# Mixture of experts: scatter and gather in halves between a neighbouring expert's units, h cast on ACT

## The reference, cut to what matters

```python
def _moe_swiglu(x, w_router, b_router, w_gate, w_up, w_down):
    logits = (x @ w_router).astype(jnp.float32) + b_router.astype(jnp.float32)
    top_vals, top_idx = lax.top_k(logits, TOP_K)          # TOP_K = 2
    top_w = jax.nn.softmax(top_vals, axis=-1)
    combine = jnp.sum(jax.nn.one_hot(top_idx, N_EXPERTS, dtype=jnp.float32) * top_w[..., None], axis=-2)
    out = jnp.zeros_like(x)
    for e in range(N_EXPERTS):                            # N_EXPERTS = 8
        out = out + combine[..., e:e + 1].astype(x.dtype) * _swiglu(x, w_gate[e], w_up[e], w_down[e])
    return out
```

## Time and profile before

| | us |
|---|---|
| median of 3 runs | 3123.27 |
| lowest and highest | 3120.66, 3128.55 |
| span of the profiled execution | 3126.1 |
| busy: PE, DVE, ACT | 2690.1, 2311.1, 1477.0 |
| start of the expert layer (first gather) to its last scatter | 1978 to 3108 |

### The profile page before, as it was taken

How to read it: one execution, slowest core, us unless ns; L and a number is a source line. 1 busy time by engine, 2 the same in 40 slices (tenths; PEclk the granted TensorE clock), 3 DMA queues, 4 the chain that set the end, 5 groups by cost and what they waited for, 6 DMA issues and landing times.

```text
span 3126.1 us, 48237 instructions
## 1 busy us (share of the span) xinstructions
PE 2690.1 (86%) x17714; PEld 2431.0 (78%) x17715; DVE 2311.1 (74%) x2670; ACT 1477.0 (47%) x1605; POOL 950.9 (30%) x566
## 2 busy tenths in 40 slices
PE   7998689899888987568996656799999989998997
PEld 7987489899888886347996534698888979897896
DVE  5666466667668656867777686698888979897897
ACT  4333443433343333125552212476666767666665
POOL 6960069599209002317996321000000000000000
PEclk9988699899898998688997778799999999999999
DMA  7753157477344442025752203497978969896985
GB/s 279 253 182 142 41 215 257 172 257 255 134 182 141 168 161 106 27 101 210 261 207 85 101 31 118 158 359 299 343 277 298 361 261 359 307 363 258 344 310 195
DMA packets 128885, 670.36 MB, mean 214 GB/s; under 512 B 14496, under 2 KB 14688, under 8 KB 79632
## 3 DMA queue, kind: packets, MB, share of 16 engines
q1 hardware_dynamic: 110848, 604.72, 52.6%
q0 software_dynamic: 17936, 64.18, 5.9%
HBM read 667.80 MB, written 1.05 MB: 214 GB/s over the span
## 4 chain that ended last, share of the span: by engine, by line
PE 78%; DVE 14%; issue 3%; ACT 3%; POOL 1%; DMA 1%; DVEq 0%; SPq 0%; ACTq 0%
PE work L1372 15%; PE work L1373 15%; PE work L1374 15%; PE acc L1372 9%; PE acc L1373 8%; PE acc L1374 8%; PE acc L1720 1%; PE work L1712 1%; DVE scratch L1049 1%; PE acc L1735 1%; PE work L1420 1%; DVE wl_gu L644 1%; PE work L1449 1%; DVE xT_lo L731 1%; DVE wl_gu L1142 1%
## 5 line engine op out<-in xcount | busy, mean ns | idle before, releaser
L1372 PE MATMUL work<-xT_hi,wh_gu 128*128 128x256 f32 x2120 | 613.6, 289 | 54.9 <-DVE xT_lo L731 19.6
L1373 PE MATMUL work<-xT_lo,wh_gu 128*128 128x256 f32 x2120 | 611.2, 288 | 0.0
L1374 PE MATMUL work<-xT_hi,wl_gu 128*128 128x256 f32 x2120 | 610.2, 288 | 0.0
L1372 PE MATMUL work<-wh_gu,mixT_hi 128*128 128x256 f32 x1792 | 510.3, 285 | 10.5 <-DVE wl_gu L1142 9.7
L1373 PE MATMUL work<-wl_gu,mixT_hi 128*128 128x256 f32 x1792 | 505.9, 282 | 0.0
L1374 PE MATMUL work<-wh_gu,mixT_lo 128*128 128x256 f32 x1792 | 505.8, 282 | 0.0
L644 DVE TENSOR_TENSOR wl_gu<-raw_gu,wh_gu 128x2048 fp32r<-128x2048 f32 x158 | 394.8, 2499 | 133.9 <-ACT wh_gu L351 133.3
L1372 PEld LDWEIGHTS work<-xT_hi,wh_gu 128*128 128x128 f32 x2120 | 417.9, 197 | 66.5 <-DVE xT_lo L731 21.9
L1373 PEld LDWEIGHTS work<-xT_lo,wh_gu 128*128 128x128 f32 x2120 | 418.3, 197 | 4.7
L1374 PEld LDWEIGHTS work<-xT_hi,wl_gu 128*128 128x128 f32 x2120 | 417.9, 197 | 0.0
L1372 PE MATMUL acc<-wh_d,h_hi 128*128 128x512 f32 x912 | 382.2, 419 | 4.1 <-DVE wl_d L1147 4.1
(11 more groups left out here) (417 smaller groups left out, 4942.1 us busy)
## 6 DMA issues: line engine op xcount, KB each, us to landing
raw_gu<-in_w_gu SPq DMA_DIRECT2D x271, 1024.0 KB, 4.9
raw_d<-in_w_d SPq DMA_DIRECT2D x269, 512.0 KB, 5.3
scratch<-in_w_gu SPq DMA_DIRECT2D x112, 1024.0 KB, 7.1
scratch<-in_w_d SPq DMA_DIRECT2D x112, 512.0 KB, 7.9
scratch<-in_w_mod POOLq DMA_DIRECT2D x96, 512.0 KB, 3.7
scratch<-in_s_b POOLq DMA_DIRECT2D x16, 256.0 KB, 3.0
rows<-in_norm_post POOLq DMA_DIRECT2D x6, 512.0 KB, 3.9
rows<-in_ln_g POOLq DMA_DIRECT2D x4, 512.0 KB, 4.0
```

The costliest lines, as they stand in the source:

```text
L1372: pe.matmul(out_, w[0], m[0], start=start, stop=False)
L1373: pe.matmul(out_, w[0], m[1], start=False, stop=False)
L1374: return pe.matmul(out_, w[1], m[0], start=False, stop=stop)
```

## The change

**PE.** The transposes and the scatter of the predecessor move into the expert: `scatter_previous(e, 0)` behind unit 3, `(e, 1)` behind unit 5, the transposes behind unit 7. The gather for the next expert is cut into two halves behind units 16 and 17. Scatter, transposes and gather now all use banks 2 and 3 of `work`. Behind gate_up(27) follow h_transpose(26), down(25), h_transpose(27), down(26), down(27) without anything between. The counts of both experts of a pair are loaded at the top of the pair loop. More units are written out: 0 to 7 and 16 to 19, with loops of 2 x 4 between and behind them.

**ACT** takes over the cast of h (`h_hi`), between silu and the cast of the gate and up weights. `gathered` comes in halves, behind units 17 and 18. At the end it does `moe_hi_d(27)`, the h cast, `moe_hi_gu(29)`.

**DVE** loses that cast in the sparse form; adds a scattered half behind units 3 and 5 (`add_scattered`), copies the weights behind unit 7 (`keep_weights`) and makes the low part of the tokens in halves behind units 18 and 19. The one-hot matrices are made at the top of an expert as before, those with weights for e instead of e + 1. The semaphores count halves. Before the loop there is no scatter of zeros any more; it falls on units 3 and 5 of expert 0. The final scatter is as before.

The diff, cut to the sparse form; the dense form gets the same insertions behind units 1, 2, 3 and 16 to 19.

```diff
@@ ACT @@
+            def gathered(i, half, e=0):
+
+                done = 2 * e + (2 * i + half + 1)
+                act.wait_ge(moe_s["gathered"], done)
...
+                for k in range(4 * half, 4 * half + 4):
...
+                act.activation(XGH[i % 2][:, 4 * half:4 * half + 4, :], XGF_K[:, 4 * half:4 * half + 4, :],
+                               ACT.Copy).then_inc(moe_s["xg_h"], 1)
...
+                def h_hi(i, at):
+
+                    k = (N0 + i) % 2
+                    act.wait_ge(moe_s["hT"], at + (i + 1))
+                    act.activation(HH[k][:, 0:P], PA[:, 2 + k, 0:P], ACT.Copy).then_inc(moe_s["hh"], 1)
+
+                def sparse_step(i, at, first=False):
+
+                    silu(i, at, P)
+                    if not first:
+                        h_hi(i - 1, at)
                     if i < NF2 - 1:
                         moe_hi_gu(i + 2, at)
                         moe_hi_d(i, at)
-                    else:
+
+                def sparse(e, r, pair):
+                    at = e * NF2
+                    sparse_step(0, at, first=True)
+                    for i in range(1, 8):
+                        sparse_step(i, at)
+                    with act.Fori(0, 2) as j:
+                        for i in range(8, 12):
+                            sparse_step(i, at + j * 4)
+                    sparse_step(16, at)
+                    sparse_step(17, at)
+                    gathered(r + 1, 0, pair * 2)
+                    sparse_step(18, at)
+                    gathered(r + 1, 1, pair * 2)
+                    sparse_step(19, at)
+                    with act.Fori(0, 1) as j:
+                        for i in range(20, 24):
+                            sparse_step(i, at + j * 4)
+                    for i in range(24, NF2):
+                        sparse_step(i, at)
+                    moe_hi_d(NF2 - 1, at)
+                    h_hi(NF2 - 1, at)
+                    moe_hi_gu(NF2 + 1, at)
@@ DVE @@
-                def split(i, at, src, width):
+                def h_lo(i, at, src, width):
 
                     k = (N0 + i) % 2
-                    dve.tensor_copy(HH[k][:, 0:width], src).then_inc(moe_s["hh"], 1)
                     dve.wait_ge(moe_s["hh"], at + (i + 1))
...
+                def add_scattered(e, t):
+
+                    dve.wait_ge(moe_s["scattered"], 2 * e + (t + 1))
+                    dve.wait_ge(moe_s["acc"], 2 * e + (t + 1))
+                    TT(ACC[:, t, :], ACC[:, t, :], tile2(PB[:, 2:4, :]), ALU.add).then_inc(moe_s["acc"], 1)
+
+                def keep_weights(e):
+                    dve.wait_ge(moe_s["wT"], e + 1)
+                    dve.tensor_copy(WGT_T, PB[:, 2, 0:S]).then_inc(moe_s["wT_sb"], 1)
...
+                    for i in range(1, 9):
+                        sparse_step(i, at)
+                        if i in (3, 5):
+                            add_scattered(e, (i - 3) // 2)
+                        if i == 7:
+                            keep_weights(e)
+                    with dve.Fori(0, 2) as j:
+                        for i in range(9, 13):
                             sparse_step(i, at + j * 4)
-                    for i in range(NF2 - 3, NF2):
+                    for i in range(17, 21):
+                        sparse_step(i, at)
+                        if i in (18, 19):
+                            xg_lo(r + 1, i - 18, pair * 2)
+                    for i in range(21, NF2):
                         sparse_step(i, at)
@@ PE @@
+                def scatter_previous(e, t):
+
+                    if t == 0:
+                        pe.wait_ge(moe_s["y"], e + 1)
+                        pe.wait_ge(moe_s["wT_sb"], e + 1)
+                    else:
+                        pe.wait_ge(moe_s["acc"], 2 * e + 2)
+                    scatter(t, PB[:, 2:4, :]).then_inc(moe_s["scattered"], 1)
+
+                def weights_transpose(e):
+                    pe.wait_ge(moe_s["onehots"], e + 2)
+                    pe.wait_ge(moe_s["acc"], 2 * e + 3)
...
+                    step(3, at)
+                    scatter_previous(e, 0)
+                    step(4, at)
+                    step(5, at)
+                    scatter_previous(e, 1)
+                    step(6, at)
+                    step(7, at)
+                    weights_transpose(e)
+                    with pe.Fori(0, 2) as j:
+                        for i in range(8, 12):
+                            step(i, at + j * 4)
+                    step(16, at)
+                    pe.wait_ge(moe_s["wT_sb"], e + 2)
+                    gather(0)
+                    step(17, at)
+                    gather(1)
+                    step(18, at)
+                    step(19, at)
+                    with pe.Fori(0, 2) as j:
+                        for i in range(20, 24):
+                            step(i, at + j * 4)
                     h_transpose(NF2 - 1, at)
                     slot_down(NF2 - 2, at, False, False)
                     slot_down(NF2 - 1, at, False, True)
...
                 with pe.Fori(0, NE // 2) as pair:
+                    counts = [pe.value_load(members[:, bass.ds(pair * 2 + r, 1)], min_val=0, max_val=S)
+                              for r in range(2)]
                     for r in range(2):
                         e = pair * 2 + r
-                        pe.wait_ge(moe_s["onehots"], e + 2)
-                        for t in range(NT):
-                            last = pe.transpose(PB[:, (N0 + 1) % 2, (2 + t) * P:(3 + t) * P], WGT[:, t], ident)
-                        last.then_inc(moe_s["wT"], 1)
-                        pe.wait_ge(moe_s["y"], e + 1)
-                        pe.wait_ge(moe_s["wT_sb"], e + 1)
-                        scatter()
-                        pe.wait_ge(moe_s["xg_l"], e + 1)
-                        count = pe.value_load(members[:, bass.ds(e, 1)], min_val=0, max_val=S)
-                        with pe.If(count <= P):
+                        pe.wait_ge(moe_s["xg_l"], 2 * e + 2)
+                        with pe.If(counts[r] <= P):
                             sparse(e, r)
```

More of the change, by code:

```diff
@@ L582, in moe, with silu @@
                 moe_hi_gu(1)
-                gathered(0)
-                def step(i, at, width):
+                gathered(0, 0)
+                gathered(0, 1)
+                def silu(i, at, width):
                     n = N0 + i
@@ L593, in step, with dense @@
+                def dense(e, r, pair):
+                    at = e * NF2
+                    def step(i, at):
+                        silu(i, at, S)
+                        moe_hi_gu(i + 2, at)
                         moe_hi_d(i, at)
-                        moe_hi_gu(i + 2, at)
-                def steps(e, width):
-                    with act.Fori(0, NF2 // 4 - 1) as j:
+                    with act.Fori(0, 4) as j:
                         for i in range(4):
-                            step(i, e * NF2 + j * 4, width)
-                    for i in range(NF2 - 4, NF2):
-                        step(i, e * NF2, width)
+                            step(i, at + j * 4)
+                    for i in range(16, 20):
+                        step(i, at)
+                        if i in (17, 18):
+                            gathered(r + 1, i - 17, pair * 2)
+                    with act.Fori(0, 2) as j:
+                        for i in range(20, 24):
+                            step(i, at + j * 4)
@@ L603, in moe @@
                 with act.Fori(0, NE // 2) as pair:
+                    counts = [act.value_load(members[:, bass.ds(pair * 2 + r, 1)], min_val=0, max_val=S)
+                              for r in range(2)]
                     for r in range(2):
                         e = pair * 2 + r
-                        count = act.value_load(members[:, bass.ds(e, 1)], min_val=0, max_val=S)
-                        with act.If(count <= P):
-                            steps(e, P)
-                            gathered(r + 1, pair * 2)
+                        with act.If(counts[r] <= P):
+                            sparse(e, r, pair)
@@ L612, in moe @@
                         with act.Else():
-                            steps(e, S)
-                            gathered(r + 1, pair * 2)
+                            dense(e, r, pair)
             act.wait_ge(cols_in, 16)
@@ L1151, in moe @@
                 moe_lo_gu(1)
[L1152 to L1153 removed]
+                xg_lo(0, 0)
+                xg_lo(0, 1)
                 def gated(i, at, width):
@@ L1795, in dense @@
-                    wide_gate_up(3, at)
-                    wide_down(2, at, False, False)
-                    with pe.Fori(0, (NF2 - 4) // 4) as j:
-                        for i in range(4, 8):
-                            wide_gate_up(i, at + j * 4)
-                            wide_down(i - 1, at + j * 4, False, False)
-                    pe.wait_ge(moe_s["onehots"], e + 3)
-                    gather()
+                    wide_gate_up(1, at)
+                    pe.wait_ge(moe_s["y"], e + 1)
```

(16 more changed lines are left out.)

139 lines of the change are left out of this document (70 added, 69 removed).

## The result

The kernel after takes 3148.16 us at the median (3143.53 to 3151.22), the kernel before 3123.73 beside it. The ratio is 1.0067, 95% interval 1.0050 to 1.0084: slower by 0.67%, some 21 us. The profiled execution has a span of 3149.4, 23.3 more than before's 3126.1. The traces shown were taken at a mean granted clock of 0.91 to 0.92; only that of e12 was at 0.635, in a run of 3961 us, which is left out of its time.

A forecast was written before the change was run, and what follows sets the result against it. PE bounds the kernel inside experts and waits for code between them; seams inside pairs +3.2, loop-backs +8.4, last tail +1.0 and start -3.0 gave +9.6 us, so 3133 us, range 3111 to 3150.

The forecast's parts named there:

- forecast case: Whole kernel: the summed terms hold and the time is 3125 to 3141 us; chance 0.50.
- code stalls of ACT and DVE: Rival at the seams: ACT's and DVE's longer written-out code makes them wait for code too, 3146 us; chance 0.16.
- idle time before the first gate_up: PE between experts: 2.26 us inside a pair and 9.46 at loop-backs kept, plus 0.1 and 2.0 added.
- half clock behind it: PE's slow clock after a seam's idle time: 1.1 us inside a pair, 1.75 at a loop-back.
- tail stalls: PE at an expert's end waits for `wl_d`, 0.7 us before down(26) and 0.8 before down(27).
- gather, scatter, transposes in the stream: Pieces moved between PE's units still cost 7.3 us an expert, plus 0.2 for a late silu: 7.5.
- cast on ACT: Each sparse unit: h's cast moved from DVE to ACT costs zero, with 0.9 us of cover left.
- first gather to the first expert's third gate_up: Start of the expert layer: gate_up(2) comes at 1997.0 instead of 2003.94, -6.9 us.
- the value loads: Top of PE's pair loop: two exposed loads of the counts, with the wait and the If, +2.0 us each loop-back.
- The shorter code stall: Rival at PE's loop-back: the code fetch costs only as much as the jump and the clock stays up, 3112 us; chance 0.13.
- The clock did not stay up: Rival at the seams: the clock stays up after the shorter seams, 3123 to 3127 us, no change; chance 0.15.
- late in every unit: Rival in each unit: ACT or DVE becomes late for PE, 3155 us at 0.1 us past the cover; chance 0.06.

The follow-up runs named there:

- e12: e9 with PE told the jump's target two units before each expert's end: 0.9922 of the kernel before.
- e7: Kernel before with only the sparse units' cast of h moved from DVE to ACT, one step late: ratio 1.0006 to the kernel before.
- e5: Kernel after, SP holding loads from unit 4 of each next expert until PE did its first gate_up tile: 0.9998 of the kernel before.
- e6: Kernel before with the same hold of SP's loads as e5: 0.9969 of the kernel before.
- e3: Kernel before with ACT's and DVE's sparse units written out instead of looped, PE untouched: 0.9999 of the kernel before.
- e10: Kernel after with PE's loop over pairs of experts written out and e5's hold of SP's loads: 0.9937 of the kernel before.
- e8: Kernel before with PE's loop over pairs of experts written out four times: 0.9938 of the kernel before.
- e2: Kernel after with the branch and the dense form taken out on ACT and DVE, PE keeping it: 1.0060 of the kernel before.
- e4: Kernel after with PE's value load once an expert, behind its wait for tokens, instead of two per pair: 1.0087 of the kernel before.
- e9: Kernel after with PE's loop over pairs of experts written out four times: 0.9995 of the kernel before.
- e11: e8 with PE told the jump's target ahead of the tail's gather: 0.9854 of the kernel before, median 3085.6 us.

## Why the prediction was right in sign and small in size

The forecast was 3133 and +9.6 us; measured were 3148 and +23.3 between the profiles. That 3148 lies in the stated range of 3111 to 3150 is in part luck: the forecast case ended at 3141, and the upper end was set for a rival (code stalls of ACT and DVE) that turned out not to be the cause. Point by point, between the third gate_up of the first expert and that of the last (seven periods, before 975.0, after 1002.2: +27.2, forecast +11.6):

| step | forecast | measured |
|---|---|---|
| idle time before the first gate_up, sum of 7 | +6.4 | +17.8 |
| half clock behind it, sum of 7 | 9.7 in all | 16.4 (before 11) |
| tail stalls, each expert | 0.7 + 0.8 | 0.49 + 0.65 |
| gather, scatter, transposes in the stream | 7.5 | 7.25 |
| cast on ACT | 0 | 0 (e7: ratio 1.0006) |
| steady unit | 4.37 | 4.37 |
| first gather to the first expert's third gate_up | -6.9 | -6.8 (25.5 to 18.8) |
| last expert's third gate_up to the end | +4.9 | +6.5 (147.1 to 153.6) |

The three stretches add up to the 26.9 (-6.8, +27.2, +6.5). Inside an expert PE stayed the bound: from 2137 to 2250 in after it is busy for all of the 113.00 us at PEclk 1.00, DVE for 98.36 and ACT for 81.52. Slips of the forecast's arithmetic are small beside this: 1.1 for the clock is called a mean of 0 and 1.7, which is 0.85; the loop-backs' +8.4 is 8.2 by its own figures; and the start of the very first gate_up, 1985.09 + 1.5 + 0.6 + 0.65, is 1987.8, not 1988.1.

**The step that failed** is the sentence "2.26 and 9.46 idle are kept. Nothing covers them." The mechanism behind it (PE waits for code, and moving the scatter doesn't change that) was right; the term was mis-sized. I took a duration of the jump from before as if it belonged to the branch. It belonged to the branch *at an idle DMA*, and the change took away what made the DMA idle there. The rows held a hint: the kernel before had a window at DMA 0.34 over the loop-back seam, which the prediction notes and does not use. That window is too wide to show more, since it takes in the jump with its quiet queues and the loop-back with full ones. Inside the pairs idle time came to 4.68, 4.01, 3.37 and 3.74 where 2.3 was forecast: 15.8 in sum against 8.3 before, 7.1 more than the 0.4 I had added. At the loop-backs 13.0 to 13.5 came: 10.3 more than before, where I had added 6.0. That makes the 11.4 us that the idle term lacked. The loop-back's own branch did not grow, and the 2.0 for the value loads fit what e5 and e6 leave between them (1.7). What was missing is the jump ahead of it, 1.1 to 2.0 us longer at the three loop-backs, where the jumps inside the pairs are 1.3 to 2.2 longer.

**The clock** was the second mis-sized term. I took 1.1 inside a pair and 1.75 at a loop-back. In the kernel after, each seam had a half-clock stretch; their sum, idle time in it included, rose from 41 to 61 us, and the cost, taken as half of PE's busy time inside them, rose from 11 to 16.4. The seams with the longer idle time, the loop-backs, had the longer stretches: 13.7 us against 3.4 to 6.8 inside pairs, where before had 10.2, and none to 3.4. Inside the pairs alone there is no such order (4.68 us idle with a stretch of 3.4 behind it, 3.37 and 3.74 with 6.8). At the first seam inside a pair the stretch (PEclk 0.50) began at 2127.7 in before, 0.3 us behind the start of the transposes, and at 2124.2 in after, 0.2 us behind the start of gate_up(0), whose matmuls took 0.41 to 0.46 us there against 0.28 to 0.29 in a steady unit. So an idle us cost about 1.3 us (17.8 + 5.4 for 17.8 more).

**The rivals.** The shorter code stall (3112) was the opposite of what came: no long branch fell under 4 us except the last, with no loads left. The clock did not stay up at any seam, and ACT and DVE were not late in every unit (4.37 us, as before). ACT and DVE stalling for code did happen: q14 went from 24 packets to 73, and in the layer DVE has three waits by "issue" before its one-hots, 16.0 us together, and ACT three before silu, 12.4. The prediction took DVE's short loop-back (56 ns at most) as a sign that its code is held; in after DVE's branches stay as short and it stops behind them all the same. But PE was late then anyway. In e3 ACT has 9.9 us of such waits and the time is that of before, and in e10 DVE has 10.3 and ACT 9.7 and the time is that of e8. I gave that rival 3146, close to the time that came; the runs speak against its reason.

## What to carry to other kernels

In this kernel PE's long jumps and loop-backs waited for a packet of code, and their price depended on what else was in the DMA queues at that moment (3.3 to 3.9 against 4.6 to 5.9 us for the same jump, e5 and after). Before moving work that stands ahead of such a branch, look up the DMA share in the window around it. Where a loop's body is long and its branches cost several us with the bound engine idle, try writing the loop out and telling the engine the target early: here the first was worth 0.6% and both 1.5%, more than the order of the work around it.

## What the runs showed of the hardware

- PE's jump past `dense`: 3.3 to 4.3 us with the data queues nearly empty (busy for 0.00 to 0.38 of the 2 us behind the branch; up to 5.0 in e7, where two packets of code were fetched), 4.3 to 6.7 with weight packets in them (0.91 to 1.02; after, e2, e4, e9). The loop-back: 6.9 to 7.9 us in before and after (6.1 to 9.0 over all runs that leave the loads alone), and 4.6 to 5.0 with them kept away. At the jumps with one packet of code, its 16 KB take 0.9 to 1.7 us; the rest is spent ahead of it and behind it.
- A branch whose target was told ahead of a 3.6 us gather (e11: 8.2 to 8.3 us before it) took 0.40 to 0.43 us, in seven of eight cases; in the eighth it took 3.75. A packet of code started 3.6 to 7.0 us ahead of the seven and none ahead of the eighth; why that one failed wasn't settled.
- ACT's and DVE's branches at the same places took 0.03 to 0.06 us in the kernel after, though q14 fetched 73 packets of code over the span (24 in before). Their stops (three of 4.9 to 5.6 us on DVE, three of 3.7 to 4.6 on ACT) stand behind the branches, not in them.
